# Converted pairs of an FFN: products that add up in PSUM, 17 of 22 pairs converted, and two down tiles side by side

## The reference, cut to what matters

```
def swiglu_ffn(h, w_gu, w_down):
    gate, up = jnp.split(h @ w_gu, 2, axis=-1)      # 1024 -> 2 x 2816
    return (jax.nn.silu(gate) * up) @ w_down         # 2816 -> 1024
x = x + 0.5 * swiglu_ffn(rms_norm(x, norm_g), w_gu, w_down)
```

## Time and profile before

| | us |
|---|---|
| median of 3 runs | 2178.5 (2178.32 to 2178.51) |
| span of the profiled execution | 2176.6 |
| around the span, to the median | 1.9 |
| PE busy | 2159.6 |
| VectorE busy | 1589.7 |
| ScalarE busy | 1093.2 |
| GpSimd busy | 284.1 |

### The profile page before, as it was taken

The page is one execution under the profiler, slowest core; times in us unless marked ns, Lnnn a source line. Parts: engine busy times, 40 slices in busy tenths (PEclk is TensorE's granted clock), DMA queues, the critical chain, the costliest instruction groups (busy, mean ns, idle before and its releaser), DMA issues.

```text
span 2176.6 us, 31752 instructions
## 1 busy us (share of the span) xinstructions
PE 2159.6 (99%) x12728; PEld 1814.8 (83%) x12728; DVE 1589.7 (73%) x2449; ACT 1093.2 (50%) x1716; POOL 284.1 (13%) x244
## 2 busy tenths in 40 slices
PE   9999999999999999999999999999999999999999
PEld 7889897777778898988899997777788898977777
DVE  6779586988657696865787777777667795965873
ACT  5535254667545252435344346777545252538672
POOL 3101013000131011131010122000131010130000
PEclk9999999999999999999999999999999999999999
DMA  7556454131136666443755452222135565532211
GB/s 213 145 136 158 118 136 136 40 98 59 59 93 168 172 156 159 109 139 83 193 117 149 115 143 95 75 76 95 50 87 159 125 161 126 134 109 78 78 59 39
DMA packets 250235, 252.58 MB, mean 116 GB/s; under 512 B 5776, under 2 KB 236304, under 8 KB 250088
## 3 DMA queue, kind: packets, MB, share of 16 engines
q1 hardware_dynamic: 207184, 206.06, 29.6%
q0 software_dynamic: 41664, 40.05, 12.1%
q10 hardware_dynamic: 1240, 4.43, 0.5%
HBM read 213.79 MB, written 6.32 MB: 101 GB/s over the span
## 4 chain that ended last, share of the span: by engine, by line
PE 90%; DVE 5%; ACT 3%; DMA 1%; issue 1%; POOL 0%; SPq 0%; DVEq 0%; ACTq 0%
PE ps L1950 89%; DVE sb_wlo L1315 1%; PE ps L1954 1%; ACT sb_whi L765 1%; DMA sb_raw<-w_ada 0%; DVE sb_gla_ek L1656 0%; DMA sb_ffn_al<-sb_ffn_u 0%; DVE sb_gla_eq L1659 0%; ACT sb_xh L765 0%; DMA sb_xT<-xT 0%; DVE sb_xT L1444 0%; ACT sb_hyb_th L765 0%; DVE sb_gla_xb L1651 0%; DVE sb_gla_cf L1648 0%; DVE sb_gla_d L1636 0%
## 5 line engine op out<-in xcount | busy, mean ns | idle before, releaser
L1950 PE MATMUL ps<-sb_xh,sb_whi 128*128 128x512 f32 (+1 forms) x1888 | 679.1, 360 | 1.8 <-DVE sb_xl L1739 0.8
L1950 PE MATMUL ps<-sb_xl,sb_whi 128*128 128x512 f32 (+1 forms) x1888 | 662.6, 352 | 0.6 <-DVE sb_xl L1335 0.6
L1950 PE MATMUL ps<-sb_xh,sb_wlo 128*128 128x512 f32 (+1 forms) x1888 | 660.4, 352 | 0.0
L765 ACT ACTIVATE sb_whi<-sb_raw 128x1024 fp32r<-128x1024 f32 (+1 forms) x368 | 378.8, 1034 | 379.8 <-PE ps L1950 366.1
L1950 PEld LDWEIGHTS ps<-sb_xh,sb_whi 128*128 128x128 f32 x1888 | 357.2, 189 | 66.7 <-issue 18.5
L1315 DVE TENSOR_TENSOR sb_wlo<-sb_raw,sb_whi 128x1024 fp32r<-128x1024 f32 (+1 forms) x256 | 332.7, 1303 | 100.1 <-ACT sb_whi L765 98.6
L1950 PEld LDWEIGHTS ps<-sb_xl,sb_whi 128*128 128x128 f32 x1888 | 357.5, 189 | 50.8 <-DVE sb_xl L1335 3.5
L1950 PEld LDWEIGHTS ps<-sb_xh,sb_wlo 128*128 128x128 f32 x1888 | 357.2, 189 | 49.1
L1950 PE MATMUL ps<-sb_ffn_ah,sb_whi 128*128 128x512 f32 x704 | 275.4, 391 | 0.8 <-DMA sb_ffn_al<-sb_ffn_u 0.8
L1950 PE MATMUL ps<-sb_ffn_ah,sb_wlo 128*128 128x512 f32 x704 | 274.1, 389 | 0.0
L1950 PE MATMUL ps<-sb_ffn_al,sb_whi 128*128 128x512 f32 x704 | 273.9, 389 | 0.0
(11 more groups left out here) (293 smaller groups left out, 2838.2 us busy)
## 6 DMA issues: line engine op xcount, KB each, us to landing
sb_raw<-ffn_w_gu SPq DMA_DIRECT2D x86, 1024.0 KB, 5.2
sb_raw<-ffn_w_down SPq DMA_DIRECT2D x32, 1024.0 KB, 5.9
sb_ffn_al<-sb_ffn_u POOLq DMA_DIRECT2D x76, 256.0 KB, 4.0
sb_raw<-sb_raw POOLq DMA_DIRECT2D x56, 256.0 KB, 4.2
sb_raw<-w_ada SPq DMA_DIRECT2D x12, 1024.0 KB, 9.2
sb_raw<-ffn_w_down SPq DMA_DIRECT2D x16, 768.0 KB, 4.9
sb_raw<-gla_w_in SPq DMA_DIRECT2D x12, 1024.0 KB, 5.4
sb_raw<-diff_w_in SPq DMA_DIRECT2D x12, 1024.0 KB, 5.2
```

The lines of the kernel that those rows point to most:

```text
L765: return e.activation(out, in_, func, bias=bias, scale=scale)
L1950: return e.matmul(out, lhsT, rhs, start=start, stop=stop, skip_group_check=skip)
```

## The change

1. `FAST` takes all of j = 5 to 21 in each FFN (17 of 22): 7, 15 and 21, each the last pair of its part, are converted too.
2. A converted pair adds up in PSUM. The region `run` holds product 1, then 1 + 6, then 1 + 6 + 7; another holds 5, then 5 + 3. ScalarE copies each value that a later product would overwrite (four copies of 256 columns a pair, semaphore `t_cap`, against one copy before), PE waits for three of them before it adds the next product, and the signs of the sums of x are changed so that all adds are additions. VectorE joins in two operations of 512 columns (`join_gate`, `join_up`). `FFN_NORM`'s bank is no longer used for products.
3. The last pair of a part is joined, multiplied and split behind the part's loop, on ScalarE and VectorE, with one `w_hi` or `w_lo` ahead.
4. In every down phase the matmuls of tiles 0 and 1 alternate: for each of the part's n activations three for tile 0, three for tile 1.
5. The ring has no offset of two in FFN 3 any more, SBUF tiles are laid out anew, and some semaphores are merged.

```
-FAST = ((5, 6, 8, 9, 10, 11, 12, 13, 14, 16, 17, 18, 19, 20),) * 4
+FAST = (tuple(range(5, 22)),) * 4
 def ffn_banks(f):
-                p += 2 * (f == 3 and part == 1)
 # ScalarE, a converted pair
-                            used(w, u)
-                                w.wait_ge(sem["f_join"], 4 * i - 7)
-                            act(first_product(sums, i), psum[FFN_NORM][...], ACT.Copy).then_inc(sem["t_act"], 1)
-                            if j > k0 and j - 1 in FAST[f]:
-                                silu(j - 1)
-                            w_hi(u + 1)
-                            w_hi(u + 2)
-                            if j > k0 and tail_late(j - 1):
-                                split(j - 1)
-                            w_hi(u + 3)
+                            w.wait_ge(sem["t_prod"], 3 * i + 1)
+                            act(one_v[i % 2][:, 0, :], run[:, 0:256], ACT.Copy).then_inc(sem["t_cap"], 1)
+                            if j > k0:
+                                split(j - 1)
+                            w_hi(u + 1)
+                            w.wait_ge(sem["t_prod"], 3 * i + 2)
+                            act(four_five[:, 1, :], two_three[:, 256:512], ACT.Copy).then_inc(sem["t_cap"], 1)
+                            used(w, u + 1)
+                            act(one_v[i % 2][:, 1, :], run[:, 0:256], ACT.Copy).then_inc(sem["t_cap"], 1)
+                            w_hi(u + 2)
+                            w_hi(u + 3)
+                            w.wait_ge(sem["t_prod"], 3 * i + 3)
+                            act(four_five[:, 0, :], four[:, 0:256], ACT.Copy).then_inc(sem["t_cap"], 1)
+                            silu(j)
 # ScalarE, behind a part's loop
+                    w_hi(u)
+                    split(k0 + n - 1)
 # VectorE, a converted pair
+                        if j > k0 and j - 1 in FAST[f]:
+                            join_up(f, j - 1, u - 4, joined, ub[(j - 1) % 2][:, :], up_free)
+                            product(j - 1, None)
                         w_lo(u)
+                        w_lo(u + 1)
+                        if j in FAST[f]:
+                            join_gate(f, j, u, joined, gb[j % 2])
+                            scale_gate(f, j, gb[j % 2])
+                            w_lo(u + 2)
+                            w_lo(u + 3)
 # VectorE, behind a part's loop
+                    join_up(f, j, u - 4, joined, ub[j % 2][:, :], up_free)
+                    product(j, None)
+                    w_lo(u)
+                    low_part(j)
 # PE, down phase
+                        if m == 0:
+                            for t in range(n):
+                                for k in range(2):
+                                    rows(u + k, t, t + 1, pair[k], H, L, ready, t == 0, t == n - 1)
+                        elif m > 1:
+                            bank_free(b)
+                            rows(u, 0, n, b, H, L, ready, True, True)
 # PE, a converted pair
+                product(run, slots[0], 0, of_x(0, early), 0, True, False).then_inc(sem["t_prod"], 1)
+                product(two, slots[0], 4, of_x(4, early), 4, True, True).then_inc(sem["w_used"], 1)
+                product(five_three, slots[1], 0, of_sums(0), None, True, False).then_inc(sem["t_prod"], 1)
+                w.wait_ge(sem["t_cap"], 4 * i + 1)
+                product(run, slots[1], 4, of_sums(2), None, False, False).then_inc(sem["w_used"], 1)
+                w.wait_ge(sem["t_cap"], 4 * i + 2)
+                product(five_three, slots[2], 0, of_x(4, late), 4, False, True).then_inc(sem["w_used"], 1)
+                product(four, slots[3], 4, of_sums(3), None, True, True).then_inc(sem["t_prod"], 1)
+                w.wait_ge(sem["t_cap"], 4 * i + 3)
+                product(run, slots[3], 0, of_sums(1), None, False, True).then_inc(sem["w_used"], 1)
```

More of the change, by code:

```diff
@@ L434, in ffn_memory @@
         def ffn_memory(f, mem):
[L435 to L438, removed]
             ah, al = sb(f"ffn{f}_ah", [128, 8, S], F32R, mem), tiles_of(sb(f"ffn{f}_al", [128, 4, S], F32R, mem))
@@ L669, in build, with halves @@
         t_before = [4 * sum(bool(FAST[k]) for k in range(f)) for f in range(5)]
-        t_act_before = [3 * t_before[f] + fast_before[f] for f in range(5)]
+        t_act_before = [3 * t_before[f] for f in range(5)]
         def tail_late(j):
             return j >= 4 and j not in (7, 15, 21)
-        def first_product(sums, i):
-            return sums[:, 12 + 2 * (i % 2):14 + 2 * (i % 2), :].rearrange("p a b -> p (a b)")
+        def halves(ap):
+            return ap.rearrange("p (k c) -> p k c", k=2)
         def ffn_banks(f):
@@ L809, in ffn @@
             def ffn(f):
-                ah, al, gb, ub, _, sums, th, _ = ffn_mem[f]
+                ah, al, gb, ub, (one_v, four_five), _, th, _ = ffn_mem[f]
                 u = first[f"ffn{f}"]
@@ L1339, in ffn @@
             def ffn(f):
-                ah, al, gb, ub, vgw, sums, th, tl = ffn_mem[f]
+                ah, al, gb, ub, joined, sums, th, tl = ffn_mem[f]
                 u = first[f"ffn{f}"]
@@ L1465, in x_sums @@
                 w.wait_ge(sem["t_vec"], 4 * n + 2)
[L1466 to L1479, removed]
+                e.scalar_tensor_tensor(out=out[:, 3, :], in0=out[:, 2, :], scalar=-1.0, in1=y[:, 2, :], op0=ALU.mult,
+                                       op1=ALU.subtract).then_inc(sem["t_vec"], 1)
@@ L1485, in join_rest @@
                 used(w, u + 3)
-                w.wait_ge(sem["f_join"], 4 * i + 1)
-                e.tensor_tensor(vgw[:, 2:4, :], vgw[:, 0:1, :].broadcast_to([128, 2, 256]), three_seven,
+                w.wait_ge(sem["t_cap"], 4 * i + 4)
+                up_free(j)
+                run = psum[f_banks[f]["pair", j][0]][:, 0:256]
+                e.tensor_tensor(halves(up), run.unsqueeze(1).broadcast_to([128, 2, 256]), joined[1][:, :, :],
                                 ALU.add).then_inc(sem["f_join"], 1)
-                w.wait_ge(sem["f_join"], 4 * i + 2)
@@ L2053, in ffn @@
                         b = f_banks[f]["down", (part, m)][0]
-                        bank_free(b)
-                        for k in range(0, n, 8):
-                            rows(u, 0, W.units[u][2], b, AH, AL, ("f_al", 22 * f + k0), k == 0, k + 8 >= n, k)
-                            u += 1
+                        H, L, ready = AH, AL, ("f_al", 22 * f + k0)
+                        if m == 0:
+                            pair = [f_banks[f]["down", (part, k)][0] for k in range(2)]
+                            for q in pair:
+                                bank_free(q)
+                            for t in range(n):
[4 more added lines that the diff above has]
+                            rows(u, 0, n, b, H, L, ready, True, True)
+                        u += 1
                         if part == len(FF_PARTS[f]) - 1:
@@ L2067, in fast_pair, with product @@
                 i = fast_before[f] + FAST[f].index(j)
-                one = psum[FFN_NORM][:, 256 * (i % 2):256 * (i % 2) + 256]
-                (six, two), (three, seven), (four, five) = ([psum[b][:, 0:256], psum[b][:, 256:512]] for b in banks)
+                run, two, four = (psum[b][:, 0:256] for b in banks)
+                five_three = psum[banks[1]][:, 256:512]
                 early, late = slice(0, 256), slice(256, 512)
-                def product(out, slot, t0, parts, ready):
+                def product(out, slot, t0, parts, ready, start, stop):
                     for t in range(4):
@@ L2078, in product @@
                         hi, lo = parts(t)
-                        mm(out, whi[slot][:, t0 + t, :], hi, t == 0, False)
-                        mm(out, whi[slot][:, t0 + t, :], lo, False, False)
-                        ins = mm(out, wlo[slot][:, t0 + t, :], hi, False, t == 3)
+                        mm(out, whi[slot][:, t0 + t, :], hi, start and t == 0, False, True)
+                        mm(out, whi[slot][:, t0 + t, :], lo, False, False, True)
+                        ins = mm(out, wlo[slot][:, t0 + t, :], hi, False, stop and t == 3, True)
                     return ins
```

103 lines of the change are left out of this document (39 added, 64 removed).

## The result

The changed kernel takes **2194.8 us** (2193.5 to 2196.4), the kernel before, on the same chip, 2178.4 (2178.3 to 2178.5): ratio 1.0076, 95% interval 1.0062 to 1.009. The forecast was 2180.1, range 2172 to 2187. No difference was thought likeliest; the kernel is slower by 0.8%. The profiled execution took 2193.5 us, span 2191.7, 15.1 us above that of before.

The account below looks back on a forecast made before the run. PE was taken to bound the kernel, busy 99% at full clock. Terms -9.96 - 1.06 + 1.23 + 2.26 + 5.17 + 4.0 = +1.6 us took the median of 2178.5 to 2180.1 us, range 2172 to 2187.

Parts of the forecast that it names:

- (b): ScalarE copies four running values per converted pair instead of one; PE would not wait for them: cost 0.
- (g): Loads in FFN 1's part 0: w_ada landing later beside the bias_rep copy, PE waiting: +4.0 us (0 to 6.3).
- (d): Converted last pair of a part: cost 0; side-by-side down tiles remove a wait in FFN 1's part 0: -1.06 us.
- (f): FFN 2's start: PE waits for bank 4, the last down tile's: +5.17 us, 2.9 by the ring alone.
- (e): Last parts: side by side delays the down tiles' chain 2.26 us: GLA +1.23, diff +2.26, FFN 3 to hybrid 0.
- (a): Twelve more converted pairs (7, 15, 21 in four FFNs), all on PE: -9.96 us.
- rival 4: Pairs converted but PE no faster, if alternating 256-column matmuls cost more than 0.120 us; chance 0.02.
- slack 0.85: In (b), the second running copy ends 0.85 us before PE needs it at a converted pair's 49th matmul.
- Rival 2: Second running copy late before the 49th matmul in every converted pair: +10.2 us, 2190; chance 0.08.
- Rival 3: Clock falls in the waits of (f) and (g): 2.6 and 2 us lost, 2184.7 us; chance 0.15.

Follow-up runs that it names:

- e1: Changed kernel with ScalarE making pair 5's first running copy ahead of pair 4's silu and the second ahead of its split: 2188.7 us, ratio 1.0047.
- e5: Changed kernel with e1, e2 and e4 together, pair 6's second copy ahead of the split, down tiles one by one in FFNs 0 to 2: 2171.3 us.
- e3: Changed kernel with all down tiles one by one in every part instead of the first two side by side: 2189.7 us, ratio 1.0051.
- e8: Kernel before with the bias_rep copy issued at pair 16 of FFN 1 instead of pair 7: 2177.5 us, ratio 0.9995.
- e6: Changed kernel with e5's edits except its last, so the first two down tiles stay side by side everywhere: 2176.0 us, ratio 0.9989.
- e2: Changed kernel with FFN 2's ring of banks begun one bank later: 2190.2 us, ratio 1.0053.
- e4: Changed kernel with the 4 MB bias_rep copy issued at pair 16 of FFN 1 instead of pair 7: 2190.2 us, ratio 1.0055.
- e7: Kernel before with the first two down tiles side by side in the last part of each FFN alone: 2185.9 us, ratio 1.0036.

## Why the prediction was wrong

Between the forecast and the median lie 14.7 us. Of these 8.1 are (b), 2.9 are (g) and (d) taken together, 1.7 the half clock behind (f), and 0.5 are (e); the median also lies 1.3 us above the profiled execution that these are read from.

(a) held to the digit, and rival 4 (no speed-up) fell with it.

**(b) is the step that failed.** Its rule was right (order counts, not busy time), and its steady times for the first two copies were right to 0.01 us. What failed is "slack 0.85", and with it "cost 0", taken for all 68 pairs: it was worked out for a converted pair behind a converted pair. Behind an ordinary pair ScalarE's queue holds that pair's silu, which waits for VectorE, and the first copy came at 71.60, where the steady rhythm gives 68.0 and PE wanted its result at 70.65. The trace of before had this row, which the forecast did not read; its pair 5 starts at 66.20, and nothing waited for it:
```profile
...
71.47 0.36 ACT L765 ACTIVATE sb_ffn_sums<-ps 128x256 f32<-128x256 f32 x1
```

Rival 2 had the mechanism but put it in every pair and at the 49th matmul alone; it bit in the first converted pair of each FFN, at both copies, 8.1 us in sum. e1 takes 5.9 of it away by order alone, and in e5, with pair 6 reordered too, the three pairs take 30.2 to 30.3 us in every FFN.

(d) The number came out for another reason than the forecast's. The wait it was to save is gone in the changed kernel, but not by the order of the tiles: it is gone one by one as well (e3), and e8 shows it to be the bias_rep copy's work. Why the copy spares it now, issued 4.4 us later, was not tried. Cost of the converted last pair in parts 0 and 1: nothing, also one by one (e3), as forecast.

(e) The chain's shift (2.26, measured 2.29 at the first evacuation) and its price at diff (+2.26, measured +2.33) held. At GLA the term was 0.4 too small: the eighth step starts at 365.61, as late as forecast, but takes 0.98 us to the next matmul instead of 0.54. FFN 3's 0 held. The forecast never asked what side by side buys: 0.7 us of waiting in a last part and nothing in the others (e3), against the price that e6 shows.

(f) The forecast was 5.17, measured 5.08; e2 and e3 confirm the split between ring and chain.

(g) The mechanism held (e4), the size did not: with (d)'s 1.06 back in, 4.79 + 1.06 + 1.08 = 6.9 us, which e4's windows give back, for a forecast of 4.0. The load was issued 3.1 us later than forecast (698.54 against 695.4) and landed as late as the upper end. PE then lost 2.4 us in two waits, 1.7 in the half clock behind them, 1.7 in late weights for pair 8 and 1.1 in the eight pairs, 0.93 of it at a late copy in pair 9. (g) had priced one wait of PE in the down phase, of up to 6.3 us, and nothing behind it.

Rival 3 came true: half clock behind (f) and in (g), 1.7 us each. By the Trainium skill (TensorE: Matmul & The Clock Gate, Part 1) an idle stretch brings the half rate back; the rows at 979.61 agree. The rival had a chance of 0.15, and its 2.6 + 2 us stood apart from the sum, although its condition, the wait of (f), was part of the sum. With a wait of 5 us forecast it belonged there. The measured time lies 7.8 us above the range, about the size of (b).

## What to carry to other kernels

When an engine that used to trail the matmuls becomes one they wait for, work its queue through at every change of rhythm (first pair behind an ordinary one, first behind a down phase), not only in the steady state. Of the 24.8 us that the account adds up beside (a)'s gain, 8.1 lay at the first converted pair of each FFN, the rest at the starts and ends of down phases and beside one large copy. Moving work, the banks and that copy, without any less work, turned +16 us into -7. A forecast PE wait of several us carries the half clock behind it as a term of the sum. A reordering that is to hide a wait must be tried alone: side by side cost 7 us in the kernel before (e7) and hid nothing there.

## What the runs showed of the hardware

Behind a wait of 2 us the half clock sometimes comes and sometimes does not. Of nine PE waits of 2.01 to 2.03 us (above the pitch) at the starts of FFN 2 and diff in six profiled executions, five were followed by three to four us at 1.2 GHz, which cost 1.2 to 1.6 us, and four were not. The changed kernel's wait at diff is one of the four; its window, beside those of e6 and e7 above:
```profile
...
1338.30:1342.00 3.70, 3.30 (x11) 2.10 (x12) 3.05 (x6) 1.35 (x3) 2.42 (x3) 1.00 0.31 112
```

The three waits of 5.08 and the one of 2.64 were followed by it (1.6 to 2.0 us each), and so were the waits in FFN 1's part 0 in all four executions that had them; no single wait of up to 1.7 us was. The spread of the times goes with it. Kernels without such waits kept within 0.5 us (before, 22 runs), 0.8 (e8) and 1.3 (e5), and every one of these runs had a mean granted clock of 1.000. Those with them went over 2.1 us (e2), 2.4 (e3), 2.8 (e7), 3.9 (e6) and 4.0 (e4); e1, with 0.8 in four runs, is the exception. e7's five runs show the steps: 2184.7 us at a mean clock of 1.000, 2185.9 twice at 0.999, 2187.5 and 2187.6 at 0.998. Why one wait of the same length brings it and the next does not was not tried.

One 4 MB copy from DRAM to DRAM, issued by another engine, made a 1 MB load on SyncE's queue take 26 us from issue to landing. Of the two loads of w_ada issued between 685 and 735 us the median was 23.8 beside the copy, and 7.6 without it. DMA issues of that stretch (count, KB each, median us to landing), the changed kernel first, then e4:
```profile
...
sb_raw<-w_ada SPq DMA_DIRECT2D x2, 1024.0 KB, 23.8
```

```profile
...
sb_raw<-w_ada SPq DMA_DIRECT2D x2, 1024.0 KB, 7.6
```

By the Trainium skill (DMA: Bandwidth & Descriptors, Issuing engines are not separate DMA queues) copies issued by different engines share the same 16 DMA engines and interleave; these rows agree.
